# Two half products in place of one: the pointwise matrix of a gated conv/attention layer on the two halves of the TensorE array

## What is computed

```python
for l in range(DEPTH_2):                      # two layers
    ...                                       # attention branch -> mla_out, 1024 wide
    u = causal_depthwise_conv(u, dw_w[l], dw_b[l])
    u = jax.nn.silu(layer_norm(u, conv_ln_g[l], conv_ln_b[l]))
    u = u @ w_pw[l] + b_pw[l]                 # (256 x 1024) @ (1024 x 1024)
    conv_out = u * jax.nn.silu(conv_gate)
    y = jnp.concatenate([mla_out, conv_out], axis=-1) @ w_out[l]
    x = x + gate * y
```

## Time and profile before

| | |
|---|---|
| median of three runs | 1891.74 us |
| the profiled execution: its own time | 1890.64 us |
| its span, first to last instruction | 1888.8 us |
| PE busy | 1878.5 us, 99% of the span |
| DVE busy | 1583.1 us, 84% |
| ACT busy | 999.9 us, 53% |
| mean share of the 16 DMA engines (main queue) | 72.5% |

### The profile page before, as it was taken

The page is one execution under the profiler, slowest core; times in us unless marked ns, Lnnn a source line. Parts: engine busy times, 40 slices in busy tenths (PEclk is TensorE's granted clock), DMA queues, the critical chain, the costliest instruction groups (busy, mean ns, idle before and its releaser), DMA issues.

```text
span 1888.8 us, 24873 instructions
## 1 busy us (share of the span) xinstructions
PE 1878.5 (99%) x9230; PEld 1589.3 (84%) x9230; DVE 1583.1 (84%) x2169; ACT 999.9 (53%) x1455; POOL 136.0 (7%) x88
## 2 busy tenths in 40 slices
PE   9999999999999999999999999999999999999999
PEld 7888888888888888888888878888888788888887
DVE  6898888888887988888887578898898788888986
ACT  6646555455444444443444464667655555667562
POOL 1232233000000000000000000001100000010000
PEclk9999999999999999999999999999999999999999
DMA  7787877889888998989897556655566466555554
GB/s 262 260 273 258 291 255 252 275 287 312 293 296 283 320 300 298 305 293 313 285 311 249 191 159 174 199 166 161 152 201 201 144 192 182 166 167 163 198 192 144
DMA packets 259195, 445.04 MB, mean 236 GB/s; under 512 B 16051, under 2 KB 123461, under 8 KB 258819
## 3 DMA queue, kind: packets, MB, share of 16 engines
q1 hardware_dynamic: 258643, 443.36, 72.5%
q10 hardware_dynamic: 432, 0.09, 0.0%
HBM read 441.27 MB, written 2.11 MB: 235 GB/s over the span
## 4 chain that ended last, share of the span: by engine, by line
PE 98%; DVE 1%; issue 0%; ACT 0%; POOL 0%; DVEq 0%; ACTq 0%
PE P L733 73%; PE P L794 12%; PE P L800 6%; PE P L505 2%; PE P L636 1%; PE P L635 1%; PE P L621 0%; PE P L547 0%; PE P L572 0%; PE P L643 0%; PE P L718 0%; PE P L654 0%; PE P L653 0%; PE P L652 0%; PE P L573 0%
## 5 line engine op out<-in xcount | busy, mean ns | idle before, releaser
L1165 ACT ACTIVATE WH<-RAW 128x1024 fp32r<-128x1024 f32 (+1 forms) x647 | 669.4, 1046 | 569.7 <-PE P L733 238.1
L1196 DVE TENSOR_TENSOR WL<-RAW,WH 128x1024 fp32r<-128x1024 f32 (+1 forms) x649 | 791.4, 1225 | 201.2 <-ACT WH L1165 198.0
L733 PE MATMUL P<-WH,AHL 128*128 128x512 f32 (+1 forms) x2048 | 642.2, 389 | 3.4 <-DVE AHL L1196 3.2
L733 PEld LDWEIGHTS P<-WH,AHL 128*128 128x128 f32 x2048 | 381.8, 188 | 79.5 <-issue 4.8
L733 PE MATMUL P<-WL,AHL 128*128 128x512 f32 (+1 forms) x1024 | 392.1, 385 | 0.0
L733 PE MATMUL P<-WH,BH 128*128 128x512 f32 x896 | 351.1, 392 | 0.0
L733 PE MATMUL P<-WH,BL 128*128 128x512 f32 x896 | 348.9, 389 | 0.0
L733 PE MATMUL P<-WL,BH 128*128 128x512 f32 x896 | 348.7, 389 | 0.0
L794 PE MATMUL P<-AHL,WH 128*128 128x512 f32 x1024 | 252.0, 392 | 0.0
L1193 DVE SCALAR_TENSOR_TENSOR ADA<-RAW,CC,ADA 128x1024 f32<-128x1024 f32 x180 | 238.5, 1325 | 1.1 <-DMA RAW<-in_ada_w_dram 1.1
L733 PEld LDWEIGHTS P<-WL,AHL 128*128 128x128 f32 x1024 | 192.4, 188 | 35.6 <-DVE WL L1196 0.4
(11 more groups left out here) (270 smaller groups left out, 1394.3 us busy)
## 6 DMA issues: line engine op xcount, KB each, us to landing
RAW<-in_ada_w_dram SPq DMA_DIRECT2D x192, 512.0 KB, 5.3
RAW<-in_mlp_w_in_dram SPq DMA_DIRECT2D x128, 512.0 KB, 5.0
RAW<-in_mlp_w_out_dram SPq DMA_DIRECT2D x128, 512.0 KB, 5.4
RAW<-in_sb_w_qkv_dram SPq DMA_DIRECT2D x95, 512.0 KB, 5.1
RAW<-in_w_in_dram SPq DMA_DIRECT2D x80, 512.0 KB, 3.9
RAW<-in_w_in_dram SPq DMA_DIRECT2D x128, 256.0 KB, 3.2
RAW<-in_w_out_dram SPq DMA_DIRECT2D x64, 512.0 KB, 4.4
RAW<-in_sb_w_o_dram SPq DMA_DIRECT2D x32, 512.0 KB, 5.4
```

The lines of the kernel that those rows point to most:

```text
L733: return e.matmul(P[:, 2 * u.pair + t, 0:u.w], x, w, start=u.first and k == 0 and part == 0, stop=u.last and k == u.nk - 1 and part == 2)
L1165: e.activation(WH[:, n % NH, 0:size], RAW[:, i % NR, 0:size], ACT.Copy).then_inc(w_high, 1)
L1196: return e.tensor_tensor(o, x, h.bitcast(F32), ALU.subtract)
```

## The change

Three parts. (1) The units of `p` are done by a function of their own, `unit_by_half`: each product of 128 rows becomes two products of 64 rows, partitions 0 to 63 and 64 to 127 of the same operands, issued in turn. The lower half sums in the group's own pair, the upper half in the other pair; so a `p` group holds all four banks. (2) `open_both` books that second pair, behind all its earlier users, and the first unit of a `p` group waits until it is emptied too. (3) `p_evict` adds the second pair: one more DVE instruction per half of the columns, between the bias and the gate; the second one frees the second pair.

```diff
+        def open_both(g, c):
+            upper[g, c] = (1 - opened[g, c][0], pairs_used[1 - opened[g, c][0]])
+            pairs_used[upper[g, c][0]] += 1
...
             def p_units(c):
                 for k in range(0, 8, 2):
                     unit(("p", l), c, A["w_pw_2"][l], k * 128, k, 2, 512 * c, 512, k == 0, k == 6)
+                open_both(("p", l), c)
...
+            def unit_by_half(n):
+                u, s = units[n], n % NH
+                if u.first:
+                    e.wait_ge(pair_emptied[upper[u.g, u.c][0]], upper[u.g, u.c][1])
+                banks = (opened[u.g, u.c][0], upper[u.g, u.c][0])
+                for k in range(2):
+                    for t in range(2):
+                        for part in range(3):
+                            for h in range(2):
+                                p = slice(64 * h, 64 * h + 64)
+                                w = (WH, WL, WH)[part][p, s, k * u.w:(k + 1) * u.w]
+                                x = low_of[u.g][part // 2][p, u.k0 + k, t * 128:(t + 1) * 128]
+                                m = e.matmul(P[:, 2 * banks[h] + t, 0:u.w], x, w, start=u.first and k == 0 and part == 0, stop=u.last and k == 1 and part == 2)
+                return m
...
                     if u.g == "m1":
                         m = turned_unit(n)
+                    elif u.g[0] == "p":
+                        m = unit_by_half(n)
                     else:
...
-                p0 = 2 * opened[("p", l), c][0]
+                p0, p1 = 2 * opened[("p", l), c][0], 2 * upper[("p", l), c][0]
                 for i in range(2):
                     x, a = slice(256 * i, 256 * i + 256), 512 * c + 256 * i
                     e.tensor_tensor(MP[:, :, x], P[:, p0:p0 + 2, x], spread(BR[:, a:a + 256]), ALU.add).then_inc(
                         *((pair_emptied[opened[("p", l), c][0]], 1) if i else p_bias.up(l, c)))
                     e.wait_ge(*(emptied(("p", l), c) if i else p_bias.at(l, c)))
+                    e.tensor_tensor(MP[:, :, x], P[:, p1:p1 + 2, x], MP[:, :, x], ALU.add).then_inc(
+                        *((pair_emptied[upper[("p", l), c][0]], 1) if i else p_upper.up(l, c)))
+                    e.wait_ge(*((pair_emptied[upper[("p", l), c][0]], upper[("p", l), c][1] + 1) if i else p_upper.at(l, c)))
                     e.tensor_tensor(MP[:, :, x], MP[:, :, x], SCG[:, :, a:a + 256], ALU.mult).then_inc(*p_gated.up(l, c, i))
```

More of the change, by code:

```diff
@@ L210, in build @@
         units, done, after, pairs_used, side = [], {}, defaultdict(list), [0, 0], [0]
-        opened = {}
+        opened, upper = {}, {}
         def unit(g, c, src, r0, k0, nk, c0, w, first, last, pair=None):
@@ L465, in build @@
         mx, ex, rcp, o_high = tally("score_max"), tally("score_exp"), tally("score_recip"), tally("o_high")
-        conv_d, x_mid, p_bias, p_gated = tally("conv"), tally("x_half_added"), tally("p_biased"), tally("p_gated")
+        conv_d, x_mid, p_bias, p_upper, p_gated = tally("conv"), tally("x_half_added"), tally("p_biased"), tally("p_upper_added"), tally("p_gated")
         ln_d, ln_a, ln_p, ul_high, ul_low, gact = tally("ln_dve"), tally("ln_square"), tally("ln_rstd"), tally("ul_high"), tally("ul_low"), tally("gate_silu")
@@ L470, in build @@
                    lnexp, tn_mask, a_exp, a_mask, bh_high, rstd_sq, hid_part, hid_sq, hid_high, hid_low, pads, tabs, sig, lat_sq, lat_ms, lat_r, lat_high,
-                   kr_sq, kr_ms, kr_rot, q_sq, q_ms, q_rstd, q_rot, rot, k_sq, k_ms, k_rs, k_nrm, k_rope, rope_zero, x_scaled, x_scaled_a, mx, ex, rcp, o_high, conv_d, x_mid, p_bias, p_gated,
+                   kr_sq, kr_ms, kr_rot, q_sq, q_ms, q_rstd, q_rot, rot, k_sq, k_ms, k_rs, k_nrm, k_rope, rope_zero, x_scaled, x_scaled_a, mx, ex, rcp, o_high, conv_d, x_mid, p_bias, p_upper, p_gated,
                    ln_d, ln_a, ln_p, ul_high, ul_low, gact, p_high, x_done]
```

## The result

The changed kernel takes 1934.94 us (median of four runs, 1934.42 to 1936.98), the kernel before 1891.74 beside it (median of four runs, 1891.48 to 1891.91). The ratio is 1.023, with a 95% interval of 1.0219 to 1.0242: 43 us slower, at the forecast of 1935. The profiled execution took 1934.84 us, its span grew from 1888.8 to 1933.0, by 44.2 us.

What follows compares the result with a forecast made beforehand. PE was taken to bound the kernel, with no slack. Halves 0, waits 30.3, clock 13.0 and the rest 1.0 sum to 44.3 us over 1890.64, so 1935 us; range 1921 to 1983.

Steps and rivals of the forecast that it cites:

- Part 1: In the `p` products, two half products side by side cost what one whole product did, 0.2267 us; adds 0.
- The lower end, 0: For the 192 split `p` products: halves side by side add nothing; the upper end was 43.5 us.
- sign 1: In the trace, half products of one array half start about 0.227 apart if side by side, 0.454 if one after the other.
- one after the other: Rival: the two halves of each `p` product run in sequence, adding 43.5 us, so 1978.5 us; chance 0.32.
- Part 2: PE waits for DVE to free the second pair before `p` 0, `p` 1 and `ob` 0; 30.3 us in all.
- sign 2: PE waits for DVE on L1622's line twice, 7.3 to 7.7 us, and on the new addition's line four times, 3.6 to 4.2.
- Sign 4: `ob` 1 and all behind it run as before.
- Part 3: Behind PE's stands the granted clock falls to half; five falls of 2.6 us taken, 13.0 us, from 5.2 to 15.6.
- Sign 3: The clock falls to 0.50 behind each stand and is back some 5 us after PE restarts; the count tests 13.0.
- Part 4: Remaining effects, chiefly PE's changes between whole-array and half-array work: 0 to 1.3 us, 1.0 taken.
- the forecast's own range: Total time if halves run side by side, with waits and clock falls: 1921 to 1942 us; chance 0.59.

Runs made afterwards that it cites:

- two moved evictions: Changed kernel with the `oa` 3 eviction one step up in DVE's order, 1930.56 us; two steps up, with all PSUM reads before the gates, 1915.32 us.
- filled kernel: Changed kernel with whole products that nobody reads put into PE's stands, 32 ahead of `p` 0, 15 ahead of `p` 1 and `ob` 0: 1924.20 us.
- two filled kernels: Changed kernel with stands filled by products that nobody reads: with half products 1924.20 us, with whole products over two pairs 1922.28 us.
- lower-only kernel: Changed kernel without the upper 64 rows of each `p` product, stands not filled: 1968.19 us.
- the reads first: Changed kernel with `p_evict` doing both bias additions and both second-pair additions before the gates: 1927.61 us.
- the last kernel: Changed kernel with the `oa` 3 eviction two steps up in DVE's list and all PSUM reads before the gates in `p_evict`: 1915.32 us.
- kernels with halves in turn: Changed kernel with each unit's twelve lower half products before its twelve upper ones: 2012.77 us; the same with stands filled by unread products: 1948.72 us.

## Why the prediction was right

**Part 1, the halves: right.** The lower end, 0, was the true one: pairs are 0.227 us apart (sign 1 of "What would show it"), and leaving the upper halves out changes the stage by 0.1 us. Two 64-row products cost one whole product, and so the split gains nothing. The 0.32 for "one after the other" was a large chance for a case that no run showed at alternate halves. The Trainium skill ("TensorE: Matmul & The Clock Gate", Part 3, The mechanism) has products on distinct row groups run together, and the runs agree. Its start distance of some 4 ns is met by 114 of the 192 pairs (2 to 7 ns); the others have 12 to 37 ns, at the same 0.227 us from pair to pair.

**Part 2, the waits: right, and by its own mechanism.** Expected were stands of 7.5, 7.6 and four times 3.8, 30.3 us; measured 7.44 twice and 3.72 four times, 29.8. The waits stand on the lines of sign 2, 7.3 us twice and 3.6 us four times, at the lower edge of what it allowed. (By its own rows the 7.6 of layer 1 should have been 7.7: 7.49 and 0.2.) Whole products on two pairs reproduce them, the two moved evictions shorten them by what their place in DVE's order gives. One sentence was too short, though right for this change: that nothing ahead of the `oa` 3 reads waits for PE. What paces them is ACT, and it showed only when the reads were moved. Sign 4 held too: from the end of the fall behind `ob` 0 to the end of layer 0 the products lie as before.

**Part 3, the clock: right in kind and in sum, off in its terms.** It said five falls of 2.6 us, 13.0. There were seven stretches at half rate, 13.6 us at most, 1.9 each: six behind the six stands (every short one counted), one at the layer border that nothing had pointed to and that cost 0.6 us. The price of one went from 1.6 to 2.9: behind three of the four short stands the fall comes late (3.7 to 4.6 us after PE went quiet, not 2.7) and only some 3.4 us of work is done at half rate (1.6 us lost), where the prediction had gone by 5.2 us at the program's start. The filled kernel, with 10.7 us less, confirms the size. Sign 3, back some 5 us after PE starts again, held within 3.4 to 6.1 us.

**Part 4, the rest: right in size.** 1.0 us was taken, from 0 to 1.3. Between the two filled kernels sixteen changes cost 1.5 us; in the changed kernel, which has twelve, the comparison with whole products on two pairs leaves some 1.0. The Trainium skill ("TensorEngine Tiling (Array Packing)", Key Properties) says that a change of the tiling mode drains the engine, and these 1.5 us in sixteen changes agree with it.

**The sum.** 29.8 of stands, 12.6 of clock (13.6, less the 1.0 that the border did not cost) and 1.0 of passage make 43.4, where 44.2 were measured. The 0.8 that are left are of the size of a term that the prediction did not have: behind a stand the second product follows the first after 0.33 us and not 0.23 (1451.84 to 1452.17), 0.1 us at each of six stands. No run takes this term apart. That the forecast came to within 0.1 us is therefore partly luck: the stands and the clock were each forecast some 0.5 us too high, and about as much was missing. The range, up to 1983, was wide for the sake of a case that is now excluded; the forecast's own range of 1921 to 1942 would have held it.

## What to carry to other kernels

Splitting the rows of a product over the two halves of the array brings no rate where whole products are already spaced by their columns; it is paid in banks, and where the banks were given out in turn, a group that takes all of them turns every eviction beside it into a stand of PE. So ask of a change on the array first which bank it waits for, and read the end of the last read of that bank in the evicting engine's order; that gave 67% of this loss, 29.8 of 44.2 us, to within 2%. Then price each stand twice, once for its length and once for the clock behind it, even if it is only 2 to 4 us long.

## What the hardware showed that was not expected

- **A halved clock did not recover on half the array.** At 64 rows per product alone PE worked for the rest of the stage at 0.50 in both layers (some 87 us of work in the lower-only kernel), and the clock returned 2.9 and 5.4 us after whole products began. With both halves at work it returned 3.4 to 6.1 us after PE started again, and a clock that was full stayed so on the lower half alone (11 us at a time, between fillings). What decides this inside the chip stays open.
- **Short stands for an eviction do bring the clock down.** In the changed kernel all four of 3.72 us did, with the reads first two of four of 2.74, and in the last kernel two of four of 2.74 and one of two of 2.14. These are counts of one execution each, and the length doesn't decide alone: the waits at the layer border (1.0 and 1.9 us) are in all thirteen kernels, and the clock fell there in nine of them, and not in the kernel before. The Trainium skill ("TensorE: Matmul & The Clock Gate", Loop structure matters more than you think) notes for a copy out of PSUM by DVE that it doesn't break the warm state, in a loop whose next products follow at once; here the next products waited for just such reads, and these stands did.
- **Products of the other half overtake.** In the kernels with halves in turn the first product of the other half started together with the ninth of twelve, ahead of three that stand before it in the order (1439.23 beside 1439.22). The Trainium skill ("TensorE: Matmul & The Clock Gate", Part 3, The mechanism) calls products strictly ordered in start and end; these records differ for products on different halves. At alternate halves the order never showed.
